# First output projection of a two-layer decoder in split products, with a new order at the begin and in the router

## What is computed

```
h = x
for layer in (0, 1):
    q, k, v, qc = rms_norm(h) @ w_in          # 0: 12 query heads, 3 key/value heads; 1: 12 and 12
    self = sliding-window attention with sinks and rotary (0) | stick-breaking attention (1)
    cross = attention of 4 heads over rms_norm(mem) @ w_mem_kv
    h = h + rms_norm(concat(self, cross) @ w_out)
    y = swiglu(rms_norm(h)) (0: dense, width 3584) | top-2-of-8 experts, each such a swiglu (1)
    h = h + rms_norm(y)
```

## Time and profile before

| what | us |
|---|---|
| median of 3 runs (lowest, highest) | 1462.42 (1461.78, 1463.46) |
| the profiled execution's own time | 1462.98 |
| its span, first to last instruction | 1461.3 |
| PE, DVE, ACT, POOL busy | 1435.8, 1141.4, 968.8, 108.0 |
| begin, attention and first projection of layer 0 | 0 to 119 |
| dense layer | 119 to 365 |
| attention of layer 1, router | 365 to 497 |
| experts, 8 jobs, and the end | 497 to 1461 |

### The profile page before, as it was taken

The page is one execution under the profiler, slowest core; times in us unless marked ns, Lnnn a source line. Parts: engine busy times, 40 slices in busy tenths (PEclk is TensorE's granted clock), DMA queues, the critical chain, the costliest instruction groups (busy, mean ns, idle before and its releaser), DMA issues.

```text
span 1461.3 us, 19200 instructions
## 1 busy us (share of the span) xinstructions
PE 1435.8 (98%) x6979; PEld 1186.4 (81%) x6979; DVE 1141.4 (78%) x841; ACT 968.8 (66%) x818; POOL 108.0 (7%) x186
## 2 busy tenths in 40 slices
PE   6999999999999999999999999999999999999998
PEld 6957888888998888888888888888888888888886
DVE  4756444555555798989898899989898999888997
ACT  4445334433566677777787787787778778777775
POOL 3002000001000540010010010010001001000001
PEclk9999999999999999999999999999999999999999
DMA  9608565553643599999999999999999999999995
GB/s 339 225 1 310 193 203 173 175 200 130 217 140 120 171 384 378 365 392 381 372 376 390 375 366 397 369 360 400 380 358 388 389 368 383 384 375 361 381 381 187
DMA packets 177742, 446.92 MB, mean 306 GB/s; under 512 B 8800, under 2 KB 19104, under 8 KB 161568
## 3 DMA queue, kind: packets, MB, share of 16 engines
q1 hardware_dynamic: 173584, 432.08, 81.0%
q0 software_dynamic: 4112, 14.22, 2.8%
HBM read 438.37 MB, written 7.90 MB: 305 GB/s over the span
## 4 chain that ended last, share of the span: by engine, by line
PE 90%; DVE 3%; ACT 3%; issue 2%; DMA 1%; SPq 0%; POOL 0%; ACTq 0%; DVEq 0%
PE psum L479 27%; PE psum L481 27%; PE psum L480 27%; PE psum L602 2%; PE psum L1048 2%; ACT w_hi L1230 2%; DMA raw<-in_l_w_in 1%; DVE w_lo L1643 1%; PE psum L441 1%; PE psum L777 0%; PE psum L768 0%; PE psum L960 0%; PE psum L701 0%; PE psum L1080 0%; PE psum L835 0%
## 5 line engine op out<-in xcount | busy, mean ns | idle before, releaser
L1643 DVE TENSOR_TENSOR w_lo<-raw,w_hi 128x2048 fp32r<-128x2048 f32 x378 | 861.9, 2291 | 180.6 <-ACT w_hi L1230 179.3
L1230 ACT ACTIVATE w_hi<-raw 128x2048 fp32r<-128x2048 f32 x378 | 724.6, 1919 | 270.7 <-PE psum L481 270.6
L479 PE MATMUL psum<-w_hi,x_hi 128*128 128x512 f32 (+2 forms) x1216 | 476.7, 392 | 4.1 <-DVE w_lo L1643 2.6
L481 PE MATMUL psum<-w_hi,x_lo 128*128 128x512 f32 (+2 forms) x1216 | 470.1, 387 | 0.0
L480 PE MATMUL psum<-w_lo,x_hi 128*128 128x512 f32 (+2 forms) x1216 | 469.3, 386 | 0.0
L479 PEld LDWEIGHTS psum<-w_hi,x_hi 128*128 128x128 f32 x1216 | 228.4, 188 | 51.7 <-DVE w_lo L1643 5.5
L481 PEld LDWEIGHTS psum<-w_hi,x_lo 128*128 128x128 f32 x1216 | 228.3, 188 | 46.0
L480 PEld LDWEIGHTS psum<-w_lo,x_hi 128*128 128x128 f32 x1216 | 228.7, 188 | 43.1
L479 PE MATMUL psum<-w_hi,h_hi 128*128 128x512 f32 x576 | 225.4, 391 | 0.0
L481 PE MATMUL psum<-w_hi,h_lo 128*128 128x512 f32 x576 | 224.2, 389 | 0.0
L480 PE MATMUL psum<-w_lo,h_hi 128*128 128x512 f32 x576 | 224.1, 389 | 0.0
(11 more groups left out here) (266 smaller groups left out, 956.7 us busy)
## 6 DMA issues: line engine op xcount, KB each, us to landing
raw<-in_l_w_gate SPq DMA_DIRECT2D x126, 1024.0 KB, 7.3
raw<-in_l_w_up SPq DMA_DIRECT2D x126, 1024.0 KB, 7.7
raw<-in_l_w_down SPq DMA_DIRECT2D x126, 1024.0 KB, 7.0
raw<-in_l_w_in SPq DMA_DIRECT2D x10, 1024.0 KB, 5.8
raw<-in_l_w_out SPq DMA_DIRECT2D x8, 1024.0 KB, 6.7
raw<-in_l_w_in SPq DMA_DIRECT2D x6, 768.0 KB, 15.8
raw<-in_l_w_mem_kv SPq DMA_DIRECT2D x4, 1024.0 KB, 7.4
ys<-mixT SPq DMA_DIRECT2D x4, 512.0 KB, 6.6
```

Of the source, the lines that this page charges most:

```text
L479: pe.matmul(out, x[0], w[0], start=first, stop=False, skip_group_check=True)
L481: return pe.matmul(out, x[1], w[0], start=False, stop=last, skip_group_check=True)
L1230: act.activation(w_hi[:, m % CUT, :], raw[:, n % RAW, :], ACT.Copy).then_inc(hi_ok, 1)
L1643: dve.tensor_tensor(w_lo[:, m % CUT, :], raw[:, n % RAW, :], w_hi[:, m % CUT, :].bitcast(F32), ALU.subtract).then_inc(lo_ok, 1)
```

## The change

- **Begin.** The gains of the memory's and x's norms come as single rows of 4 KB on ACT's DMA queue. PE multiplies a column of ones by each row, so that PSUM holds the broadcast: for the memory's in full float32, for x's as high and low part, made by ACT and DVE. DVE multiplies rows by root and by that PSUM. The turn of x stands after the first half of the memory product, x is lowered ahead of the second cut. The zeros come from another tile, set by POOL after the rotary part, and SP stores them after weight piece 15; DVE waits for them ahead of the first post-norm.
- **Projection.** Its weight pieces A, B, C and half of D (k 4 and 5) are cut into `w_hi`, `w_lo`, `h_hi` and `h_lo`; k 6 and 7 of the right half stay in full float32. A and B are k 0 to 3 and 4 to 7 of the left 512 columns, C and D those of the right ones. For self-attention units ACT writes the high part from PSUM in `mixed`, and DVE the low part in `mix_lower`, in step u + 3 ahead of the row maximum. POOL splits the two units of memory attention from ACT's copy. PE does all of tile 0 first, then tile 1, with the turn of tile 0's rows ahead of its last ten products.
- **Dense layer.** Its rows are multiplied by the gains alone; the inverse root enters as the scale of SiLU and as third operand of the product with the up part. Its pieces 0 and 1 are cut after the first post-norm.
- **Router.** 2 filler products instead of 8 ahead of the turns, then 5 and 3 instead of 6 and 4 after each turn, and 3 new ones after the logits of tile 0; ACT drains tile 0 ahead of its cut.

```diff
-BASE1 = CUT0 + NPC
+OUT0 = 2 + CUT0
+OUT0_CUTS = ("A", "C", "B", "D")
+OUT0_LOAD = {"A": OUT0, "B": OUT0 + 1, "C": OUT0 + 2, "D": OUT0 + 3}
+OUT0_SLOT = {"A": 1, "C": 2, "B": 0}
+OUT0_COUNT = {x: CUT0 + n + 1 for n, x in enumerate(OUT0_CUTS)}
+BASE0 = CUT0 + len(OUT0_CUTS)
+BASE1 = BASE0 + NPC
...
-        zeros = mixT[:, 0:4, :].rearrange("p k s -> p (k s)")
+        zeros = xn[:, 0, :]
...
+                    for tt in range(NT):
+                        pe.wait_ge(*bk.empty(("mem0T", tt, half)))
...
                         end(ins, ("kmT", layer))
-                        turn(PRE0, "x0T", (0, 1, 2, 3))
                     for tt in range(NT):
                         for k in ks:
                             ins = pe.matmul(bank(banks[1], tt * 256, (tt + 1) * 256),
                                             srcT[:, k, tt * P:(tt + 1) * P], w.at(k, 256, 512),
                                             start=(tt == 0 and k == 0), stop=(k == KD - 1),
                                             skip_group_check=True)
+                    if half == 0:
+                        turn(PRE0, "x0T", (0, 1, 2, 3))
...
+            pe.wait_ge(ones_ok, 1)
+            pe.wait_ge(gain_row_in[MEM0], 16)
+            for hf in range(2):
+                begin(("gain", MEM0, hf), 6 + hf)
+                ins = pe.matmul(bank(6 + hf), ones[0:1, :], gains[0:1, MEM0, hf * 512:(hf + 1) * 512],
+                                start=True, stop=True)
+                end(ins, ("gain", MEM0, hf))
+            pe.wait_ge(row_hi, 2)
+            pe.wait_ge(row_lo, 1)
+            for hf in range(2):
+                begin(("gain", PRE0, hf), 4 + hf)
+                for n, x in enumerate(row_parts):
+                    ins = pe.matmul(bank(4 + hf), ones_r, x[:, hf * 512:(hf + 1) * 512],
+                                    start=(n == 0), stop=(n == 1), skip_group_check=True)
+                end(ins, ("gain", PRE0, hf))
             pe.wait_ge(ident_ok, 1)
             turn(MEM0, "mem0T", (0, 1, 2, 3))
-            turned("mem0T")
             memory_kv(0, memT, (6, 7))
...
-            n_raw[0] = 2 + CUT0
-            head_k, memory_k = range(2 * NKV), range(2 * NKV, KD)
-            w = {hf: Block() for hf in range(2)}
-            for i in range(NKV):
-                pe.wait_ge(*bk.empty(("o", UNITS0[NT * i][0])))
-            mix_part(0, 0, w, head_k, 0)
+            def split_units(n):
+                pe.wait_ge(mix_lowered, min(n, 2 * NKV))
+                if n > 2 * NKV:
+                    pe.wait_ge(mix_split, n - 2 * NKV)
+            def out_part(tt, hf, ks):
+                label = ("mix", 0, tt, hf)
+                for k in ks:
+                    first, last = k == out_first[tt], k == KD - 1
+                    if first:
+                        begin(label, 2 * tt + hf)
+                    x = "AC"[hf] if k < 4 else "BD"[hf]
+                    ts = slice(tt * P, (tt + 1) * P)
+                    if x == "D" and k >= 6:
+                        n = OUT0_LOAD["D"]
+                        pe.wait_ge(raw_full[n % RAW], 16 * (n // RAW + 1))
+                        ins = pe.matmul(bank(2 * tt + hf), mixT[:, k, ts], raw_at(n, 4, FB)[:, k - 4, :],
+                                        start=False, stop=k == out_last[tt], skip_group_check=True)
+                    else:
+                        pe.wait_ge(lo_ok, OUT0_COUNT[x])
+                        w = [y.rearrange("p (c n) -> p c n", n=FB)[:, k % 4, :] for y in out0_parts(x)]
+                        ins = thrice(bank(2 * tt + hf), [y[:, k, ts] for y in (x_hi, x_lo)], w, first,
+                                     k == out_last[tt])
+                    if k == out_last[tt]:
+                        end(ins, label)
+                return ins
+            out_first, out_last = (0, 4), (KD - 1, None)
+            split_units(5)
+            out_part(0, 0, range(4))
+            out_part(0, 1, range(4))
             weigh_unit(UNITS0[-2])
             turn_unit(UNITS0[-1])
-            for i in range(NKV):
-                pe.wait_ge(*bk.empty(("o", UNITS0[NT * i + 1][0])))
-            mix_part(0, 1, {0: w[0]}, head_k, 2)
+            for hf in range(2):
+                out_part(0, hf, (4, 5))
             weigh_unit(UNITS0[-1])
-            pe.wait_ge(*bk.empty(("o", UNITS0[-2][0])))
-            mix_part(0, 0, w, memory_k, 0)
-            pe.wait_ge(*bk.empty(("o", UNITS0[-1][0])))
-            mix_part(0, 1, {0: w[0]}, memory_k, 2)
-            mix_part(0, 1, {1: w[1]}, range(KD - 1), 2)
+            split_units(7)
+            for hf in range(2):
+                out_part(0, hf, (6, 7))
+            out_last = (KD - 1, 3)
+            split_units(8)
+            ins = out_part(1, 0, range(4, KD))
+            ins.then_inc(used, 1)
+            n_used[0] += 1
+            out0_free["B"] = (used, n_used[0])
+            out_part(1, 0, range(4))
+            out0_free["A"] = bk.full(("mix", 0, 1, 0))
+            out_part(1, 1, (4, 5))
             turn(FPRE0, "f0T", (4, 5, 6, 7), [0])
-            mix_part(0, 1, {1: w[1]}, [KD - 1], 2)
+            out_part(1, 1, (6, 7))
+            out_part(1, 1, range(4))
+            out0_free["C"] = free_after[OUT0_LOAD["D"]] = bk.full(("mix", 0, 1, 1))
...
-            keep_running(8)
+            keep_running(2)
             pe.wait_ge(small_in, 16 * 3)
             begin(("logits",), 0)
             for tt in range(NT):
                 turn(FPRE1, "f1T", (2, 3, 6, 7), [tt])
-                keep_running((6, 4)[tt])
+                keep_running((5, 3)[tt])
                 turned("f1T", tt)
                 for k in range(KD):
                     ins = pe.matmul(bank(0, tt * NE, (tt + 1) * NE), xT[:, k, tt * P:(tt + 1) * P],
                                     wr[:, k, :], start=(k == 0), stop=(k == KD - 1))
+                if tt == 0:
+                    keep_running(3)
...
             def mixed(u, i, tt):
+                if i < NKV:
+                    act.wait_ge(*bk.full(("o", u)))
+                    act.activation(mix0(i, tt)[0], bank(bk.at["o", u][0], 0, 256).rearrange("p (c s) -> p c s", c=2),
+                                   ACT.Copy).then_inc(mix_high, 1)
+                    return
...
+                    if s == len(units):
+                        cut_high_out("B")
                     if s == len(units) + 1:
-                        cut_high0(0)
-                        cut_high0(1)
+                        cut_high_out("D")
...
+            def cut_high_out(x):
+                n = OUT0_LOAD[x]
+                act.wait_ge(raw_full[n % RAW], 16 * (n // RAW + 1))
+                if x != "D":
+                    act.wait_ge(*cut0_free[{"A": 4, "C": 5, "B": 7}[x]])
+                act.activation(out0_parts(x)[0], out0_raw(x), ACT.Copy).then_inc(hi_ok, 1)
...
+            for norm in (MEM0, PRE0):
+                act.dma_start(gains[0:1, norm, :], t[NORMS[norm]].rearrange("(a d) -> a d", a=1))\
+                    .then_inc(gain_row_in[norm], 16)
+            act.wait_ge(ones_ok, 1)
+            act.activation(ones_r, ones[0:1, :], ACT.Copy).then_inc(row_hi, 1)
+            act.wait_ge(gain_row_in[PRE0], 16)
+            act.activation(row_parts[0], gains[0:1, PRE0, :], ACT.Copy).then_inc(row_hi, 1)
...
             cut_high_in(0)
+            for tt in range(NT):
+                raise_turned("x0T", tt)
             cut_high_in(1)
             copy(("kmT", 0), kmT, bank(6).rearrange("p (c s) -> p c s", c=2))
-            for tt in range(NT):
-                raise_turned("x0T", tt)
             cut_high_in(2)
...
+            cut_high_out("A")
+            cut_high_out("C")
             attend(UNITS0)
...
             post_norm(POST0, 0, ("mix", 0), spare)
+            cut_high0(0)
             pre_norm(FPRE0, 0, 0)
+            cut_high0(1)
             raise_turned("f0T", 0)
...
-                    act.activation(act0[:, tt, :], bank(bk.at[label][0]), ACT.Silu)\
+                    act.activation(act0[:, tt, :], bank(bk.at[label][0]), ACT.Silu, scale=root(FPRE0, tt))\
...
+            drain_rows(0)
             cut_high1(0, 1)
-            drain_rows(0)
...
+            def mix_lower(u, i, tt):
+                hi, lo = mix0(i, tt)
+                dve.wait_ge(mix_high, u + 1)
+                dve.tensor_tensor(lo, bank(bk.at["o", u][0], 0, 256).rearrange("p (c s) -> p c s", c=2),
+                                  hi.bitcast(F32), ALU.subtract).then_inc(bk.empty_sem(("o", u)), 1)
+                dve.wait_ge(*bk.empty(("o", u)))
+                dve.sem_inc(mix_lowered, 1)
             def attend(units):
                 for s in range(len(units) + 2):
+                    if s >= 3 and units[s - 3][2] < NKV:
+                        mix_lower(*(units[s - 3][x] for x in (0, 2, 3)))
...
+                    if s < 2:
+                        cut_rest_out("AC"[s])
...
+            def scale_first(norm, src):
+                b = bk.at["gain", norm, 0][0]
```

(63 more changed lines are left out.)

68 lines of the change are left out of this document (41 added, 27 removed).

## The result

The changed kernel takes **1471.03 us** (median of 5 runs, 1468.35 to 1471.43), the kernel before 1462.08 beside it: ratio 1.0049, 95% interval [1.0038, 1.0059]. It is slower by 0.5%, where no measurable change was forecast. The profiled execution took 1471.03, span 1468.9, so 7.6 us more than the span of before.

A forecast was written before the change was run, and what follows sets the result against it. TensorE, busy 98% of the span, was taken as the bound. Begin -2.7, attention and projection +3.6 and router -0.7 sum to +0.2 us: 1463.2 profiled, 1462.6 forecast as median, range 1458.8 to 1466.8.

The forecast's parts named there:

- a clock under 1.00 past 100 us: Whole kernel: one of the listed signs that would show the forecast wrong, TensorE's granted clock falling after 100 us.
- bound of -3.6: Begin: best case against the forecast -2.7 us, if the first 16 transposes (3.32 us) ran as fast as later ones (1.91).
- 0.42 us, with its own completion waited for 0.45: Attention: DVE's subtraction from PSUM per unit; five ahead of unit 6's turn, 5 x 0.45 = 2.25 us.
- waits for ACT: Attention: DVE's subtractions ahead of the row maximum wait for ACT's copy, 0.43, 0.56, 0.16, 0.56 and 0.50: 2.2 us.
- 0.7 of slack: Attention: DVE's present slack in the loop takes 0.7 us back, leaving PE 6.0 us later at unit 6.
- bound of 7.5: Attention: upper bound on the 6.0 us delay, if the ACT-DVE round is twice as slow in the waits.
- B's wait: Output projection: PE waits after unit 7's turn for B's low part, which DVE makes late: +3.0 us.
- rival (b): Attention and B: waits make the clock fall, each further stretch costing 2.9 us; 1467.0 us, chance 0.12.
- six fillers fewer: Router: fewer filler products ahead of the first turn let it start at 481.75, 1.35 us sooner; router in all -0.7.
- the sum of +0.2: Whole kernel: begin -2.7, attention and projection section +3.6, router -0.7, added to the profiled 1462.98 us.
- (a): Rival, attention, begin and router: the waits fit and the begin pays in full, -3.6 us, 1458.8; chance 0.24.
- (c): Rival, begin: the gain row lands late, so begin gives +2.9 instead of -2.7 us, 1468.2; chance 0.05.

The follow-up runs named there:

- router_only: The kernel before with only the new router's order and fillers: 1461.17 us, ratio 0.9996.
- begin_only: The kernel before with only the new begin; attention, projection and router as before: 1460.56 us, ratio 0.9981.
- lower_late: The changed kernel with DVE's mixed-row subtraction behind the normalising instead of ahead of the row maximum: 1464.62 us, ratio 1.0016.
- both_nowait: The changed kernel, B and D cut a step sooner, mixed-row subtraction behind the normalising, no DVE wait for its own low part: 1459.13 us, 0.9973.
- fill_b: The changed kernel with 20 identity products put in TensorE's pause ahead of block B, the wait kept: 1470.78 us, ratio 1.0045.
- begin_router: The kernel before with the new begin and new router, its attention and F32 projection unchanged: 1460.48 us, ratio 0.9984.
- cuts_early: The changed kernel with the cuts of B and D a step sooner on ACT and DVE: 1463.53 us, ratio 1.0010.
- router_back: The changed kernel with the router's order and fillers of before: 1470.96 us, ratio 1.0054.
- the best version: The changed kernel, B and D cut sooner, mixed-row subtraction behind normalising without DVE's own wait, router of before: 1458.36 us, ratio 0.9969.
- pool_all: The changed kernel with B and D cut a step sooner and all eight units' mixed rows split by GpSimd: 1460.91 us, ratio 0.9981.
- both: The changed kernel with B and D cut a step sooner and the mixed-row subtraction behind the normalising: 1459.57 us, ratio 0.9978.

## Why the prediction failed

The time, 1471.0, lies above the range (1458.8 to 1466.8), and one of the prediction's own signs of being wrong showed: a clock under 1.00 past 100 us. Two steps failed most. It put the falls of the clock at nothing in its sum, and it priced DVE's subtraction with its own wait at 0.45 us where it takes 0.63.

**The begin** was right in this profile (28.41, forecast 28.4 to 28.6). The row of x's gains, which ACT has to round first, was issued behind the memory's, at 1.28, and was there at 4.07, 2.8 us later, where I took 3.7:

```profile
4.07 1.06 ACT L1351 ACTIVATE h_hi<-gains 1x1024 fp32r<-1x1024 f32 x1 [0.95 <-DMA gains<-in_l_attn_pre_g]
```

This and what follows partly make up for each other: the second multiplication ended at 9.7 instead of 9.3, the memory products began at 12.24 instead of 12.5. The memory's own row was there at 2.68, 2.0 us after its issue, which agrees with the fixed cost by the Trainium skill's "DMA: Bandwidth & Descriptors" (Anatomy of one DMA). The bound of -3.6 had the first 16 transposes as fast as later ones if PE had worked before; PE had, from 2.68 us on, and they still took 3.65.

But the forecast was compared with a slow begin, and that the difference came out as forecast owes something to luck. In the profile of router_only, whose begin is that of before, the last thing that DVE's x rows wait for is their root, not the gains:

```profile
18.41 1.28 DVE L1558 SCALAR_TENSOR_TENSOR xn<-hres,rstd,gains 128x1024 f32<-128x1024 f32 x1 [4.78 <-POOL rstd L2038]
```

and the first split product comes at 29.37, not 31.25. Most runs of before gather near 1461.6 and 1463.7 at the same clock, which fits this 1.9 us; that they are these two begins is argued, not shown. Against the quicker one the new begin gives 0.75 by begin_only's profile (28.62), and 0.3 to 1.8 by all profiles with it, whose first split product lies between 27.54 and 29.03.

**Attention**, +7.85 instead of +6.0. The step "0.42 us, with its own completion waited for 0.45" is mis-sized: it is 0.42 + 0.21 = 0.63, five times, +0.9. The waits for ACT were 2.57 in the first five, forecast 2.2 (each a little longer): +0.4. C's cut took 2.28. The sum, 2.28 + 3.15 + 2.57, leaves 0.15 of the 0.7 of slack. The 7.85 also lies above the bound of 7.5 given for it, which doesn't follow from its own terms: waits of ACT twice as long would have added 2.2, to 8.2. lower_late and both_nowait confirm the mechanism: moved, the part gives 3.68 back, and without the own wait 1.2 more (4 x 0.30).

**The projection**: products -5.2 (forecast -5.3) and B's wait 2.98 (forecast 3.0) were right. What failed is that **the clock was kept as a rival (b) at 0.12**, when it should have been in the forecast. The row after B shows it: 1.7 to 1.8 us (39.43 less 34.76 less 2.98).

**The router**, 0.7 sooner in its order (366.00 and 366.08 against 366.71), as forecast, but +2.73 measured: the fall from 491 to 502 costs 3.4 (369.44 less 366.08). PE had no wait there in this profile: it went through transposes, fillers and 8-column products. The step "six fillers fewer" counted the fillers' time and gave what they do for the clock no price. Rival (b) looked only behind B.

Together: attention +1.85, projection +1.9 (the fall), router +3.4, the end +0.4 (the gather, still under the fall) and the begin -0.1 make the 7.4 us between the sum of +0.2 and 7.6.

Rival (b) rested partly on a misread row: the mean of 0.998 I took for falls inside the kernel, but in before the only windows under 1.00 lie at the very end (1456 us on). The conclusion from it should have been the stronger one, that before's clock never fell while it waited no longer than 1.2 us behind its first product, so that no row priced a new 3 us wait at zero. The rule of the Trainium skill, "TensorE: Matmul & The Clock Gate" (HAM oscillation), was put beside it and weighed too low; fill_b's 1.00 in the two windows agrees with it. (a) is out: the waits don't fit. (c) is out: the row of x's gains landed in 2.8 us, not 8.4.

What stays open is when a fall comes. Of ten profiled kernels with the new router seven show one in or behind it (router_only, begin_router and cuts_early don't), of four with the old none. All seven have the split products too, so with one profile each the router's part in it is likely and not shown. Five kernels of the twelve show one at 68 to 97 us, all with split products and with a DVE order or GpSimd part that makes PE wait there; the changed kernel itself, whose waits there are the same as router_back's (the longest 2.23 us in both), shows none, and neither do the four with `mix_lower` behind the normalising and no more on GpSimd than the change gives it. The changed kernel's two groups of runs, 1468.4 at clock 0.997 and 1471.2 at 0.994, also say that the same program falls once more or once less. Here more idle time of TensorE goes with more falls; a single profile doesn't say where one comes.

## What to carry to other kernels

A part moved onto an engine that paces a loop must stand where its input is already there, behind the instruction that others wait for: here the same subtractions cost 3.7 us more ahead of the row maximum than behind the normalising, where they waited for nothing. Give a new wait of TensorE of some microseconds two prices, the wait and the slower products behind it (here 3.0 and 1.8), and expect the falls to move when only one is mended. Split products were worth 5.2 us of PE but cost 3.0 in attention even when mended (58.69 against 55.72); beside the begin alone the best version gains little that intervals can tell (0.9969 [0.9957, 0.9981] against 0.9981 [0.9972, 0.9990]).

## What the runs showed of the hardware

- GpSimd and DVE hold each other up for whole instructions: a 128x4 instruction of DVE took 3.97 us beside GpSimd's 4.59, and 0.63 to 0.75 beside its 0.73. The 2.52 us that GpSimd's 128x256 took beside DVE's cuts, against 0.73 for a subtraction of that size in a quiet place, fits as the other side of it. The Trainium skill's "SBUF — State Buffer" (Who interferes with whom) states an exclusive lock on a pair of ports that DVE and GpSimd share, held for a whole instruction; these rows agree. DVE's instructions with sources in SBUF were hit; its reductions from PSUM ran at their usual 1.22 us in pool_all, one of them (76.71 to 77.93) right beside two of GpSimd.
- An F32 product of 128 columns of the identity cost 0.22 us of PE as two instructions (20 products, 4.38 us), where the expectation of fill_b had 3.0 us for all twenty.
- A wait of DVE for its own 128x256 result shows as 0.21 us of idle time and puts the next instruction 0.30 us later (0.63 us from start to start in both, 0.33 in both_nowait).
- A wait of 2.98 us of TensorE was followed by its lower clock in all three kernels that had it, and where products took its place (fill_b) it wasn't. During or behind a wait of 2.23 us the clock fell in router_back and fill_b and not in the kernel after.
